# Two transformer blocks on one Trainium2 core: feed-forward chunks with 512-wide products over the rows' high and low parts

## What is computed

```python
def swiglu(x, w_gate, w_up, w_down):            # x [256, 1024], D_FF = 2816
    return (jax.nn.silu(x @ w_gate) * (x @ w_up)) @ w_down

x = x + rmsnorm(swiglu(rmsnorm(x, g), ...), g_post)                     # f0
x = layer_norm(ALPHA * x + 0.5 * swiglu(x, ...), ln_g, ln_b)            # f1 to f4
```

## Time and profile before

| | |
|---|---|
| median of 3 runs | 1479.6 us (1475.2 to 1483.5) |
| profiled execution | 1478.82 us, span of its core 1477.3 us |
| PE | 1434.1 us busy, 97%, 10177 products |
| weight loads | 1297.4 us, 88% |
| DVE, ACT, POOL | 884.8 (60%), 735.1 (50%), 90.0 us (6%) |
| mean granted clock of PE | 0.994 |

### The profile page before, as it was taken

The page is one execution under the profiler, slowest core; times in us unless marked ns, Lnnn a source line. Parts: engine busy times, 40 slices in busy tenths (PEclk is TensorE's granted clock), DMA queues, the critical chain, the costliest instruction groups (busy, mean ns, idle before and its releaser), DMA issues.

```text
span 1477.3 us, 23985 instructions
## 1 busy us (share of the span) xinstructions
PE 1434.1 (97%) x10177; PEld 1297.4 (88%) x10177; DVE 884.8 (60%) x1167; ACT 735.1 (50%) x1045; POOL 90.0 (6%) x124
## 2 busy tenths in 40 slices
PE   7999999999999999999999999999999998999997
PEld 5888888998789988998887999889998897789986
DVE  4766656555465555797657555565565665665554
ACT  4754645444354444776325444444444476454442
POOL 3001000000000000000300000000000113200000
PEclk9999999999999999999999999999999999999999
DMA  8744637665576665530215665656667552276651
GB/s 297 242 127 161 232 94 228 186 199 190 168 226 187 197 190 184 179 116 15 87 36 188 187 199 189 213 173 188 203 197 215 168 173 84 67 239 186 204 192 71
DMA packets 121610, 253.94 MB, mean 172 GB/s; under 512 B 8040, under 2 KB 33824, under 8 KB 121376
## 3 DMA queue, kind: packets, MB, share of 16 engines
q1 hardware_dynamic: 117344, 237.60, 51.7%
q0 software_dynamic: 4160, 14.82, 3.0%
HBM read 251.34 MB, written 1.05 MB: 171 GB/s over the span
## 4 chain that ended last, share of the span: by engine, by line
PE 87%; DVE 8%; ACT 3%; issue 1%; POOL 0%; DMA 0%; SPq 0%; ACTq 0%
PE ps L1787 85%; DVE wl L1117 2%; DVE xl L1125 1%; PE ps L1885 1%; PE ps L1906 1%; ACT wh L559 1%; DVE tmp L1131 1%; ACT bsa L569 0%; ACT junk L569 0%; DVE xres L1125 0%; DMA raw<-in_w_in 0%; DVE st L1134 0%; POOL st L405 0%; ACT xh L566 0%; DVE xres L1187 0%
## 5 line engine op out<-in xcount | busy, mean ns | idle before, releaser
L1117 DVE TENSOR_TENSOR wl<-raw,wh 128x1024 fp32r<-128x1024 f32 x426 | 518.3, 1225 | 392.0 <-ACT wh L559 389.5
L559 ACT ACTIVATE wh<-raw 128x1024 fp32r<-128x1024 f32 x426 | 446.9, 1058 | 406.6 <-PE ps L1787 359.7
L1787 PE MATMUL ps<-xh,wh 128*128 128x256 f32 x1792 | 500.9, 280 | 1.7 <-DVE xl L1125 1.7
L1787 PE MATMUL ps<-xh,wl 128*128 128x256 f32 x1792 | 498.7, 278 | 0.0
L1787 PE MATMUL ps<-xl,wh 128*128 128x256 f32 x1792 | 498.6, 278 | 0.0
L1787 PEld LDWEIGHTS ps<-xh,wh 128*128 128x128 f32 x1792 | 339.3, 189 | 4.8 <-DVE xl L1125 2.3
L1787 PEld LDWEIGHTS ps<-xl,wh 128*128 128x128 f32 x1792 | 338.0, 189 | 0.3
L1787 PEld LDWEIGHTS ps<-xh,wl 128*128 128x128 f32 x1792 | 338.1, 189 | 0.0
L1787 PE MATMUL ps<-wl,fhh 128*128 128x512 f32 x368 | 143.4, 390 | 0.0
L1787 PE MATMUL ps<-wh,fhl 128*128 128x512 f32 x368 | 143.3, 389 | 0.0
L1787 PE MATMUL ps<-wh,fhh 128*128 128x512 f32 x368 | 143.3, 389 | 0.0
(11 more groups left out here) (388 smaller groups left out, 1619.3 us busy)
## 6 DMA issues: line engine op xcount, KB each, us to landing
raw<-in_ffn_w_gate SPq DMA_DIRECT2D x88, 512.0 KB, 4.0
raw<-in_ffn_w_up SPq DMA_DIRECT2D x88, 512.0 KB, 4.0
raw<-in_ffn_w_down SPq DMA_DIRECT2D x88, 512.0 KB, 4.2
raw<-in_w_out SPq DMA_DIRECT2D x24, 512.0 KB, 3.6
raw<-in_w_gate SPq DMA_DIRECT2D x22, 512.0 KB, 3.6
raw<-in_w_up SPq DMA_DIRECT2D x22, 512.0 KB, 3.7
raw<-in_w_down SPq DMA_DIRECT2D x22, 512.0 KB, 3.7
raw<-in_rwkv_w_in SPq DMA_DIRECT2D x22, 512.0 KB, 4.6
```

What stands on the lines that cost most here:

```text
L559: act.activation(slot(0, i), raw[:, i % NR, :], ACT.Copy).then_inc(act_done.new(("hi", i)), 1)
L1117: dve.tensor_tensor(slot(1, i), raw[:, i % NR, :], slot(0, i).bitcast(F32), ALU.subtract).then_inc(dve_done.new(("lo", i)), 1)
L1787: return pe.matmul(o, l, r, start=start, stop=stop, skip_group_check=True)
```

## The change

- `LOW_AT = 64`: the low weights `wl`, `fhl` and the low spare slots begin at 64 in the period of 512 bytes, high ones stay at 128. A gap tile moves for it.
- `xh` and `xl` become the halves of one tile `xs`, so one access pattern reaches both.
- `both_chunk` takes the place of `w_chunk` in chunks 1 to 5: the high weights meet both parts of the rows in one product of 512 columns, whose output is a whole bank (left half hi·hi, right half hi·lo); the low weights meet the high rows in one of 256, added to the left half. Gate has banks 0 to 3, up banks 4 to 7.
- DVE adds the halves with `halves_added`, a `tensor_reduce` over two elements that lie 256 apart, to `fhb` for gate and to `junk` for up. SiLU is then taken in place from `fhb` in SBUF, and the product reads `junk` instead of a bank.
- Chunk 0's results lie in two tiles of their own (`row_tiles`, at the ends of `fhh` and `fhl`), and its back transposes, high and low copies move from chunk 1 to chunk 5, in banks 2, 3.
- Waits: g(c) waits for DVE's "gate" of c - 1, u(c) for DVE's "up" of c - 1, `down` for "gate" of chunk 5.

```diff
-ROWS_AT, WEIGHTS_AT = 64, 128
+ROWS_AT, WEIGHTS_AT, LOW_AT = 64, 128, 64
         wh = sb("wh", [P, NH, UW], F32R)
+        sb("gap", [P, (ahead(nc.sbuf_base, LOW_AT) - nc.sbuf_base) // 4])
         wl = sb("wl", [P, NH, UW], F32R)
-        xh = sb("xh", [P, 8, T], F32R)
-        xl = sb("xl", [P, 8, T], F32R)
+        xs = sb("xs", [P, 2, 8, T], F32R)
+        xh, xl = xs[:, 0, :, :], xs[:, 1, :, :]
...
 ACT, ffn:
                 for c in range(1, 6):
-                    hi_to(after(f"f{f}g", 512 * c))
-                    act.wait_ge(*pe_done.by("ps", f"f{f}g", 512 * c))
-                    if c >= 3:
-                        act.wait_ge(*dve_done.by("hlo", f, c - 2, 1))
-                    for q in range(wide_of(c)):
-                        fn(hb[:, c % 2, q, :], ps[q][:, :], ACT.Silu, "silu", f, c, q)
-                    if c == 1:
+                    if c == 5:
                         for q in range(2):
                             act.wait_ge(*pe_done.by("back", f, q))
-                            copy(hh[:, 2 * q:2 * q + 2, :], pair(4 + q), "hhi", f, 0, q)
+                            copy(hh[:, 2 * q:2 * q + 2, :], pair(2 + q), "hhi", f, 0, q)
+                    hi_to(after(f"f{f}g", 512 * c))
+                    for q in range(wide_of(c)):
+                        act.wait_ge(*dve_done.by("gate", f, c, q))
+                        fn(hb[:, c % 2, q, :], hb[:, c % 2, q, :], ACT.Silu, "silu", f, c, q)
...
 DVE:
+            def halves_added(o, bank, *label):
+                for k in range(2):
+                    reduce(o[:, hf[k]], ps[bank + k][:, :].rearrange("p (k t) -> p t k", k=2), ALU.add, *(label if k else (*label, "first")))
...
                 for c in range(1, 6):
-                    lo_to(after(f"f{f}g", 512 * c))
-                    if c == 1:
+                    if c == 5:
                         for q in range(2):
                             dve.wait_ge(*act_done.by("hhi", f, 0, q))
-                            lower(hl[:, 2 * q:2 * q + 2, :], pair(4 + q), hh[:, 2 * q:2 * q + 2, :], "hlo", f, 0, q)
+                            lower(hl[:, 2 * q:2 * q + 2, :], pair(2 + q), hh[:, 2 * q:2 * q + 2, :], "hlo", f, 0, q)
+                    lo_to(after(f"f{f}g", 512 * c))
+                    dve.wait_ge(*pe_done.by("ps", f"f{f}g", 512 * c))
+                    if c >= 3:
+                        dve.wait_ge(*dve_done.by("hlo", f, c - 2, 1))
+                    for q in range(wide_of(c)):
+                        halves_added(hb[:, c % 2, q, :], 2 * q, "gate", f, c, q)
                     lo_to(after(f"f{f}u", 512 * c))
                     for q in range(wide_of(c)):
                         h, kt = hb[:, c % 2, q, :], slice(4 * c + 2 * q, 4 * c + 2 * q + 2)
                         dve.wait_ge(*pe_done.by("ps", f"f{f}u", 512 * c))
+                        u = junk[:, 512 * q:512 * q + 512]
+                        halves_added(u, 4 + 2 * q, "up", f, c, q)
                         dve.wait_ge(*act_done.by("silu", f, c, q))
-                        tt(h, h, ps[2 + q][:, :], ALU.mult, "mul", f, c, q)
+                        dve.wait_ge(*dve_done.by("up", f, c, q))
+                        tt(h, h, u, ALU.mult, "mul", f, c, q)
                         dve.wait_ge(*act_done.by("hhi", f, c, q))
                         lower(hl[:, kt, :], h.rearrange("p (k t) -> p k t", k=2), hh[:, kt, :], "hlo", f, c, q)
...
 PE:
+            def both_chunk(name, n0, banks):
+                kt = 0
+                for i in UNITS[name, n0]:
+                    nk, n, h, l = unit(i)
+                    pe.wait_ge(*dve_done.by("lo", i))
+                    for k in range(nk):
+                        for c in range(n // P):
+                            s = slice(c * P, c * P + P)
+                            mm(pair(banks[c]), h[:, k, s], xs[:, :, kt, :], kt == 0, False)
+                            last = mm(ps[banks[c]][:, 0:T], l[:, k, s], xh[:, kt, :], False, kt == 7)
+                        kt += 1
+                    last.then_inc(pe_done.new(("used", i), *([("ps", name, n0)] if kt == 8 else [])), 1)
...
                 for c in range(1, 6):
-                    if c > 1:
-                        pe.wait_ge(*act_done.by("silu", f, c - 1, 1))
-                    through(w_chunk(f"f{f}g", 512 * c, xh, xl, (0, 1)))
-                    if c == 1:
+                    pe.wait_ge(*(dve_done.by("gate", f, c - 1, 1) if c > 1 else act_done.by("silu", f, 0, 1)))
+                    if c == 5:
                         pe.wait_ge(*dve_done.by("mul", f, 0, 1))
                         for q in range(2):
-                            turn_rows(hb[:, 0, :, :], 2 * q, 4 + q, "back", f, q)
-                        pe.wait_ge(*act_done.by("silu", f, 0, 1))
-                    else:
-                        pe.wait_ge(*dve_done.by("mul", f, c - 1, 1))
-                    through(w_chunk(f"f{f}u", 512 * c, xh, xl, (2, 3)))
-                pe.wait_ge(*act_done.by("silu", f, 5, 0))
+                            turn_rows(lambda rb: by_rows(f, rb), 2 * q, 2 + q, "back", f, q)
+                    both_chunk(f"f{f}g", 512 * c, (0, 1, 2, 3))
+                    pe.wait_ge(*(dve_done.by("up", f, c - 1, 1) if c > 1 else dve_done.by("mul", f, 0, 1)))
+                    both_chunk(f"f{f}u", 512 * c, (4, 5, 6, 7))
+                pe.wait_ge(*dve_done.by("gate", f, 5, 0))
```

More of the change, by code:

```diff
@@ L152, in build_program @@
         gb = sb("gb", [P, 2, D])
-        at = ahead(nc.sbuf_base, ROWS_AT)
-        sb("gap", [P, (at - nc.sbuf_base) // 4])
-        xh = sb("xh", [P, 8, T], F32R)
-        xl = sb("xl", [P, 8, T], F32R)
+        at = nc.sbuf_base
+        assert at % 512 == ROWS_AT
+        xs = sb("xs", [P, 2, 8, T], F32R)
+        xh, xl = xs[:, 0, :, :], xs[:, 1, :, :]
         xf = nc.alloc_sbuf_tensor_at("xf", [P, 2, 2048], F32, offset=at)
@@ L186, in build_program @@
         qk, xqT = tmp, qkT
-        ffn_tiles = []
+        ffn_tiles, row_tiles = [], []
         for f in range(5):
-            hb, hh, hl, _ = lay(ahead(above if f < 2 else base, WEIGHTS_AT), (f"fhb{f}", [P, 2, 2, 512]), (f"fhh{f}", [P, NF, T], F32R),
-                                (f"fhl{f}", [P, NF, T], F32R))
+            hb, hh, end = lay(ahead(above if f < 2 else base, WEIGHTS_AT), (f"fhb{f}", [P, 2, 2, 512]), (f"fhh{f}", [P, NF, T], F32R))
+            hl, _ = lay(ahead(end, LOW_AT), (f"fhl{f}", [P, NF, T], F32R))
             ffn_tiles.append((hb, hh, hl))
+            ends = ahead(above if f < 2 else base, WEIGHTS_AT) + 4 * 4 * 512 + 4 * T * NF
+            row_tiles.append([nc.alloc_sbuf_tensor_at(f"fr{f}{rb}", [P, 512], F32, offset=e - 8 * T) for rb, e in enumerate((ends, ahead(ends, LOW_AT) + 4 * T * NF))])
         spare = {}
         for f, k in SPARE.items():
-            eh, el, _ = lay(TOP - 8 * UW * k, (f"{f}eh", [P, k, UW], F32R), (f"{f}el", [P, k, UW], F32R))
+            eh, end = lay(TOP - 512 - 8 * UW * k, (f"{f}eh", [P, k, UW], F32R))
+            el, _ = lay(ahead(end, LOW_AT), (f"{f}el", [P, k, UW], F32R))
             spare[f] = eh, el
@@ L321, in build_program @@
         TO_FFN = ["g0", "g1", "g2", "g3", "g4"]
+        by_rows = lambda f, rb: row_tiles[f][rb][:, :]
         wide_of = lambda c: min(512, FF - 512 * c) // T
@@ L626, in ffn @@
                     act.wait_ge(*pe_done.by("ps", f"f{f}g", 0, rb))
-                    fn(hb[:, 0, rb, :], ps[2 + rb][:, :], ACT.Silu, "silu", f, 0, rb)
+                    fn(by_rows(f, rb), ps[2 + rb][:, :], ACT.Silu, "silu", f, 0, rb)
                 hi_to(after(f"f{f}u", 0))
                 for c in range(1, 6):
-                    hi_to(after(f"f{f}g", 512 * c))
-                    act.wait_ge(*pe_done.by("ps", f"f{f}g", 512 * c))
-                    if c >= 3:
-                        act.wait_ge(*dve_done.by("hlo", f, c - 2, 1))
-                    for q in range(wide_of(c)):
-                        fn(hb[:, c % 2, q, :], ps[q][:, :], ACT.Silu, "silu", f, c, q)
-                    if c == 1:
+                    if c == 5:
                         for q in range(2):
                             act.wait_ge(*pe_done.by("back", f, q))
-                            copy(hh[:, 2 * q:2 * q + 2, :], pair(4 + q), "hhi", f, 0, q)
+                            copy(hh[:, 2 * q:2 * q + 2, :], pair(2 + q), "hhi", f, 0, q)
[3 more added lines that the diff above has]
+                        fn(hb[:, c % 2, q, :], hb[:, c % 2, q, :], ACT.Silu, "silu", f, c, q)
                     hi_to(after(f"f{f}u", 512 * c))
@@ L1238, in ffn @@
                 for rb in range(2):
-                    h = hb[:, 0, rb, :]
+                    h = by_rows(f, rb)
                     dve.wait_ge(*pe_done.by("ps", f"f{f}u", 0, rb))
@@ L1906, in turn_rows @@
                         last = pe.transpose(ps[bank][:, k * T + rb * P:k * T + rb * P + P],
-                                            src[:, rb, (c0 + k) * P:(c0 + k + 1) * P], ident)
```

(13 more changed lines are left out.)

## The result

The changed kernel takes 1510.98 us (median of 4 runs, 1507.71 to 1512.52), the kernel before on the same chip 1481.55 us (1475.2 to 1488.47): ratio 1.0205, 95% interval 1.0168 to 1.0242, 29.4 us slower. The forecast was 1487 us with a range to 1501. The profiled execution is 1507.71 us (span 1506.2), 28.9 us over that of before.

A forecast was written before the change was run, and what follows sets the result against it. TensorE's product spacing was taken to bound the kernel. Profiled 1478.8 us, plus 11.8 for waits at chunk 5, less 3.4 for the third feed-forward's slow spacing, gave 1487.2, forecast as 1487 us, range 1466 to 1501.

The forecast's parts named there:

- What bounds the kernel: Inside a feed-forward, time is the number of PE's products by their spacing; the other engines only have to keep up.
- The waits at chunk 5: PE waits for DVE's reductions, 0.7 us before u5 and 1.7 before the down product: 11.8 us for five feed-forwards.
- the walk: DVE's queue stepped through with trace durations from an up chunk's end; at chunk 5 the last gate reduction ends at 14.06.
- The reductions: On DVE, 180 reductions adding bank halves, 0.685 us each: 123 us busy, beside PE work as long as DVE keeps up.
- The rival of the strided reads: DVE's reductions read elements 1 KB apart and could cost double: 1527 to 1542 us; chance 0.08.
- I count nothing for the places: Low weights beginning at 64 instead of 128 in 512 bytes: 0 us counted; rows-stationary chunks could gain up to 1.2 us.
- A pair is 226.7 + 113.3 = 340.0: In chunks 1 to 5, one wide and one narrow product take 340.0 ns, the same as a group of three now.
- 11.8 - 3.4 = 8.4: Chunks 1 to 5: 11.8 us of waits, less 3.4 us if the third feed-forward's slow spacing doesn't come back.
- The slow spacing: Rival: new pairs in chunks 1 to 5 run at 347 ns, 10.1 us more, 1497 us; chance 0.17.
- four of five are not slow: Argument against slow pairs: of five stretches in the kernel before, one is slow and four are not.
- The cost per product: Rival: 6.7 ns paid once a product, so one fewer per group gives 9.6 us, 1478 us with the waits; chance 0.22.
- The waits did come: Rival said they don't: DVE at chunk 5 is 2 us ahead or slack is made up, leaving -3.4, 1475 us; chance 0.11.

The follow-up runs named there:

- the first experiment: The kernel before with only the low parts (weights, fhl, spare slots) moved to 64 in the 512-byte period: 1509.44 us, ratio 1.0162.
- the last kernel: Changed kernel with low parts at 128, banks freed sooner, wide products before narrow ones, high and low rows side by side, rows at 128: 1491.48 us, ratio 1.0066.
- the kernel with the halves apart: Changed kernel with low parts at 128 and banks freed sooner (1492.41 us), each wide product issued as two of 256 columns: 1477.28 us, ratio 0.9975.
- grouped products: Changed kernel with low parts at 128 and banks freed sooner, for each k all wide products first, then the narrow ones: 1483.13 us, ratio 1.0013.

## Why the prediction was wrong

**What bounds the kernel**: right. Inside a feed-forward only spacing and PE's waits counted. DVE's 105 us more cost just what stood at chunk 5.

**The waits at chunk 5**: right in place and size. In f1's chain the split on ACT starts at 529.06, so the up chunk ended at 528.96; the last gate reduction ends at 541.74 + 1.21 = 542.95, 13.99 us later, where the walk had 14.06. PE was kept from u5 for 0.7 us and from the down part for about 1.4 (1.7 forecast; the slower pairs brought PE there later). 11.8 us were forecast; about 11 is what the traces show, 10.0 and 11.9 what medians fell by when both waits were taken out, at the two places of the low parts. That one of them agrees to 0.1 us is chance.

**The reductions**: right. 682 ns each against 685 taken, DVE busy 989.7 against about 1008: reductions that follow each other overlap, so that 180 of them are busy for 57.7 + 55.9 = 113.6 us and not 123, and the weight splits are busy for 511.8 us where they were for 518.3. The rival of the strided reads falls. The Trainium skill (Advanced Engine Details and Errata, "PSUM Cachelines") asks for neighbouring elements; here elements 1 KB apart took 682 ns against 685 for the contiguous reduction of the earlier trace rows, so these reads cost nothing.

**"I count nothing for the places"**: this step failed, and it is the dearer one. It compared which two places meet in the new wide product and looked at nothing else. But the low tiles are used by the down part and by the rows-stationary chunks, which were in no need of a change. Moving them cost 9.1 us in the down part and 1.6 in chunk 0, and slowed the rows-stationary products outside the feed-forwards by the same 3.6 ns. In the kernel before, where the 256-wide groups suffer too, the places alone cost 1.6%, 24 us. The 1.2 us that the rows-stationary chunks could gain came with the other sign. The trace of before had a hint: 226.7 and 229 for the same 512-wide form, one at 128 and 128 and one at 128 and 64. It was read as a small gain and not as a sign that places set the spacing.

**"A pair is 226.7 + 113.3 = 340.0"**: failed as well. It was 346.2 on average, 8.9 us for 1440 pairs. The term took the wide product's price from the down part, where rows are stationary. In these chunks it is 226.8 in two feed-forwards of the changed kernel, 232 in three, and 235 with the low parts at 128. Place and width can't be split in these 8.9 us: at the changed kernel's places three 256-wide products take 353.3 ns or more (the first experiment), so there the pair is the faster form. The change of places alone costs the kernel before about as much (1509.44 us) as the whole change costs (1510.98).

By phases the miss is 20.5 us (1507.7 - 1487.2): 7.9 in chunks 1 to 5 (16.3 against 11.8 - 3.4 = 8.4), 9.1 in the down part, 1.6 in chunk 0, 1.9 outside.

**The rivals.** The slow spacing was the right kind, with pairs at 347 forecast and 346.2 found (an average of stretches at 350 and 340, so the nearness is luck), and was bounded at 1497 because it left the down part and the rows-stationary chunks where they were. Its argument against, "four of five are not slow", doesn't hold for a kernel whose tiles have moved. The cost per product falls: with the rows at 64, splitting each wide product in two adds 1440 products and takes 15 us away. The Trainium skill's constant of 2.5 ns a product (TensorE: Matmul & The Clock Gate, "Back-to-back issue gap") would have made that kernel slower; no run here shows such a constant. The waits did come. The range ended at 1501 since each term was bounded by rows at the old places.

**What stays open.** That places and width change the spacing is shown; why isn't. The changed kernel itself reaches 340 ns a pair in two feed-forwards of five, so the wide product is not slow by nature; with the low parts at 128 it never did, in none of the kernels run. Untested differences between a wide product at 233 and a down product at 226.8 in the last kernel are the side on which the weights are, and that in the down part the moving tile changes from product to product while here it is the same for four. What decides between 113.3 and 117.8, or between 340 and 350, from one feed-forward to the next isn't known either.

The traces do show where it changes: only where the stream of products is broken, by the eight transposes or a wait. In f1 of the changed kernel it changes at u5's wait; three pairs ahead of it and fourteen behind:

```profile
533.87 0.40 PE L1802 MATMUL ps<-xs,wh 128*128 128x512 f32 x1
...
534.92 0.39 PE L1802 MATMUL ps<-xs,wh 128*128 128x512 f32 x1
...
536.46 0.39 PE L1802 MATMUL ps<-xs,wh 128*128 128x512 f32 x1
...
541.22 0.39 PE L1802 MATMUL ps<-xs,wh 128*128 128x512 f32 x1
```

That is 350 ns a pair, then 340. In the kernel before, f2 has 340.3 ns a group in the gate half of chunk 1, ahead of the transposes, and 353.3 in everything behind them; the kernel with the halves apart has 340.1 and, in chunk 5 of f1, 353.4. In none of the 17 traces without grouped products does the spacing change inside an unbroken stretch of these chunks, which has up to 256 groups, but for its first few groups. So a stretch seems to keep the spacing that it starts with; no run set how a stretch starts, so that is not shown as a cause.

## What to carry to other kernels

A kernel whose bound is the spacing of its products pays for every tile that is moved in SBUF, also where its own code isn't touched: try the new places in the old kernel first, as a change of their own. Take the price of a product from rows with the same side stationary, the same width, the same neighbours and the same places; here that was 6 to 13 ns of 340, about 1% of the kernel. Compare two forms at the same places: the wide form loses to the narrow one at one arrangement and wins at the others measured. Read the spacing stretch by stretch, since an average over a feed-forward mixes stretches that differ. An engine with time in the sum can still be late in one short chunk, and a walk of its queue by the trace's durations finds this: the last gate reduction ended within 0.1 us of the forecast.

## What the runs showed of the hardware that was not expected

At a granted clock of 1.00, 256-wide products follow each other at 113.3, 117.8, 118.7 or 120.0 ns, and 512-wide ones with the rows stationary at 226.8 to 233.3. Which of them it is depends on the places modulo 512 bytes of the tiles they read, and at the places of the kernel before a 256-wide product can have either 113.3 or 117.8. Each is steady over an unbroken stretch and changes only at a break. A misplaced low weight tile slows also the two products of a group that don't read it. With the rows at 64 and weights and low weights at 128, a 512-wide product with the weights stationary (235 ns beside narrow ones) is slower than two 256-wide ones over the same rows (2 x 113.4), whether the rows lie in one piece or in two; with the rows at 0 or 128 a pair is faster than three 256-wide products (351.1 against 356, 352.6 against 360 ns). And a kernel whose instructions don't change can be 1.6% slower by nothing but the places of its tiles, 64 bytes less in a period of 512 for the low ones.
